# Query rounding split over two slices, gated tiles rounded inside the last attention slices, and two TensorE blocks set earlier, in a three-layer attention kernel

## The reference

```python
# layer 1 (A): windowed attention, 16 heads, context tokens too
q, k, v, g = split(h @ w_in)
q = apply_rope(q, cos, sin)            # image tokens only
p = softmax(concatenate([q @ k_window, q @ k_context, sink]))
y = ((p @ v) * silu(g)) @ w_o
# layer 2 (B): latent attention, 16 heads over all 768 keys
y = ((softmax((qn @ kn + qr @ kr) * scale) @ v) * silu(g)) @ w_o
# layer 3 (C, D): neighbourhood attention and an mLSTM, then w_out and the last norm
```

## Time and profile before

| what | us |
|---|---|
| median of 3 runs | 1173.31 |
| lowest, highest | 1172.9, 1174.43 |
| the profiled execution, its own time | 1174.93 |
| its span in the trace | 1173.1 |
| TensorE busy in it | 1105.2 |
| VectorE, ScalarE, GpSimd busy | 722.0, 652.3, 416.3 |

### The profile page before, as it was taken

One profiled execution on the slowest core, in us unless ns is written; L12 is line 12 of the kernel. 1 busy time (PEld: TensorE's weight loads), 2 busy tenths in 40 slices (PEclk: granted clock), 3 DMA queues, 4 the chain that ended last, 5 costly groups with the idle time before them and its releaser, 6 DMA issues.

```text
span 1173.1 us, 20182 instructions
## 1 busy us (share of the span) xinstructions
PE 1105.2 (94%) x7408; PEld 900.7 (77%) x7408; DVE 722.0 (62%) x1582; ACT 652.3 (56%) x1363; POOL 416.3 (35%) x512
## 2 busy tenths in 40 slices
PE   4899999999998899999999999999999999999896
PEld 0578788877886589887688888798778778887685
DVE  6365666676558625363787787645867774526545
ACT  4614455555556525643677778746567653447633
POOL 1633112211120333676400002316644335446871
PEclk9999999999989999999999999999999999999998
DMA  9741343423113621131201101043211404214112
GB/s 359 267 138 60 132 148 130 159 98 110 46 28 142 220 90 37 37 108 37 56 13 35 64 10 46 8 157 91 67 58 65 149 19 144 74 54 126 37 36 72
DMA packets 34253, 109.33 MB, mean 93 GB/s; under 512 B 4516, under 2 KB 7076, under 8 KB 33772
## 3 DMA queue, kind: packets, MB, share of 16 engines
q1 hardware_dynamic: 34156, 108.05, 27.6%
HBM read 101.39 MB, written 2.11 MB: 88 GB/s over the span
## 4 chain that ended last, share of the span: by engine, by line
PE 78%; DVE 9%; ACT 4%; issue 3%; POOL 3%; DMA 2%; SPq 0%; DVEq 0%; POOLq 0%; ACTq 0%
PE PS L675 32%; PE PS L658 15%; PE PS L791 8%; PE PS L779 7%; PE PS L970 6%; PE PS L1034 3%; PE PS L710 2%; PE PS L875 1%; DMA AF<-wstream 1%; POOL AR L2511 1%; DVE AF L2037 1%; DVE AD L2333 1%; PE PS L1009 1%; PE PS L691 1%; ACT AF L1257 1%
## 5 line engine op out<-in xcount | busy, mean ns | idle before, releaser
L2511 POOL TENSOR_TENSOR AR<-AF,AR 128x256 fp32r<-128x256 f32 x396 | 299.9, 792 | 601.0 <-ACT AR L1134 600.9
L675 PE MATMUL PS<-AR 128*128 128x512 f32 (+1 forms) x2208 | 452.3, 361 | 9.9 <-POOL AR L2511 4.1
L675 PEld LDWEIGHTS PS<-AR 128*128 128x128 f32 x2208 | 365.2, 190 | 78.0 <-issue 16.5
L658 PE MATMUL PS<-AR 128*128 128x256 f32 (+4 forms) x1284 | 246.4, 328 | 5.9 <-ACT AF L1257 1.7
L658 PEld LDWEIGHTS PS<-AR 128*128 128x128 f32 (+1 forms) x1284 | 181.0, 191 | 41.0 <-issue 20.8
L1266 ACT ACTIVATE AF<-PS 128x512 f32<-128x512 f32 (+3 forms) x192 | 124.5, 649 | 107.3 <-PE PS L779 103.3
L1257 ACT ACTIVATE AF<-PS,AF 128x512 f32<-128x512 f32 (+3 forms) x192 | 140.8, 734 | 22.0 <-DVE AF L2310 13.1
L779 PE MATMUL PS<-AF 128*128 128x128 f32 x864 | 127.8, 275 | 9.2 <-DVE AF L1958 5.8
L1134 ACT ACTIVATE AR<-AF 128x1024 fp32r<-128x1024 f32 x99 | 103.4, 1052 | 42.1 <-PE PS L970 27.8
L779 PEld LDWEIGHTS PS<-AF 128*128 128x128 f32 x864 | 100.3, 140 | 33.7 <-issue 15.1
L791 PE MATMUL PS<-AF 128*64 128x128 f32 x1728 | 115.6, 279 | 1.7 <-DVE AF L1965 1.7
(11 more groups left out here) (212 smaller groups left out, 1132.2 us busy)
## 6 DMA issues: line engine op xcount, KB each, us to landing
AF<-wstream SPq DMA_DIRECT2D x171, 512.0 KB, 4.8
AF<-x_in SPq DMA_DIRECT2D x2, 1024.0 KB, 8.1
AD<-rows SPq DMA_DIRECT2D x4, 512.0 KB, 5.9
out<-AF SPq DMA_DIRECT2D x16, 128.0 KB, 1.9
AF<-AF SPq DMA_DIRECT2D x28, 64.0 KB, 2.0
AF<-rpb_band SPq DMA_DIRECT2D x8, 224.0 KB, 5.0
BIAS<-rpb_band SPq DMA_DIRECT2D x8, 224.0 KB, 4.7
AF<-ctx_in SPq DMA_DIRECT2D x1, 1024.0 KB, 4.9
```

Of the source, the lines that this page charges most:

```text
L658: mm = pe.matmul(out, stationary, moving, start=i == 0, stop=i == len(products) - 1)
L675: mm = pe.matmul(out[:, 0:t1 - t0], a, b, start=k == 0 and i == 0, stop=k == nk - 1 and i == 2)
L2511: ins = pool.tensor_tensor(w[:, 1, at:at + 256], raw(c)[:, at:at + 256], w[:, 0, at:at + 256].bitcast(F32), ALU.subtract)
```

## The change

Five edits, in program order.

1. `ada_rows(0, 4)` on TensorE stands ahead of the fifth tile of the keys (k = 4), not behind it.
2. In layer 1, `split_image(p)` rounds the 512 image columns of the queries in `later` of slice 2, right behind `rope_q`; `split_q` of slice 3 rounds the 256 context columns alone. Pair 0 is as before.
3. At the end of layer 1's attention the first seven tiles of `A.o0.0` stand ahead of the last tile of `A.o0.1`, and the wait for the last `o_read` behind both.
4. At the end of layer 2's attention ScalarE and VectorE round the image columns' second half (part 1) of tiles 0 to 6 inside the last slices, and tile 7 and part 0 behind the last gate; TensorE starts `B.o0.1` without waiting for the last `o_read`.
5. In the iteration behind the last slice (`m == m1`), in layers 2 and 3 too, the values of the slice before are weighed between the two turnings, not behind them.

```diff
-                    if values_first and m0 <= m - behind - 1 < m1:
+                    ahead = values_first or m == m1
+                    if ahead and m0 <= m - behind - 1 < m1:
                         weigh_values(m - behind - 1)
...
-            project_together(keys, h_ready(0), 2, 5)
+            project_together(keys, h_ready(0), 2, 4)
             ada_rows(0, 4)
-            project_together(keys, h_ready(0), 5, KD)
+            project_together(keys, h_ready(0), 4, KD)
...
-            attend(0, A_END, ready_a, lambda m: fillers_a(m // 6 + 1, m % 6), values_first=True)
+            attend(0, A_END, ready_a, lambda m: fillers_a(m // 6 + 1, m % 6), values_first=True, drained=False)
+            project("A.o0.0", "A.o0", OA, 0, H, k1=KD - 1)
             make("A.o0.1:78")
-            project("A.o0.0", "A.o0", OA, 0, H)
+            project("A.o0.0", "A.o0", OA, 0, H, k0=KD - 1)
+            pe.wait_ge(o_read, group_of[A_END - 1] + 1)
...
+            def feeds_b(m):
+                if m == B_END - 2:
+                    act.wait_ge(s_ready, 2 * B_END)
+                    for j in range(2):
+                        out_high_b(j, 1)
+                if m == B_END - 1:
+                    for j in range(2, KD - 1):
+                        out_high_b(j, 1)
...
+            def split_query(p, at):
+                for half, h in enumerate(ROWS_OF):
+                    ins = dve.tensor_copy(QA[h, p % 2, half, at], QP[h, at])
+                step(ins)
+                return [dve.tensor_tensor(QA[ROWS_OF[1 - half], p % 2, half, at], QP[h, at],
+                                          QA[h, p % 2, half, at].bitcast(F32), ALU.subtract)
+                        for half, h in enumerate(ROWS_OF)]
+
+            def split_image(p):
+                dve.wait_ge(rope_sum, ropes[0])
+                if p >= 2:
+                    dve.wait_ge(s_ready, pair_scored("A", p - 2))
+                split_query(p, slice(0, S))
...
-                    dve.tensor_tensor(QA[ROWS_OF[1 - half], p % 2, half, :], QP[h, :],
-                                      QA[h, p % 2, half, :].bitcast(F32), ALU.subtract).then_inc(q_lo, 1)
+                split_query(p, slice(S, T) if p else slice(0, T))[1].then_inc(q_lo, 2)
...
                 elif s == 2:
                     rope_q(p)
+                    split_image(p)
...
+            def later_b(m):
+                if m == B_END - 1:
+                    for j in range(KD - 1):
+                        out_low_b(j, 1)
+
+            attend(A_END, B_END, others_b, later_b)
+            out_low_b(KD - 1, 1)
```

More of the change, by code:

```diff
@@ L820, in attend @@
                         turn(2 * (m - behind) + 1)
-                    if not values_first and m0 <= m - behind - 1 < m1:
+                    if not ahead and m0 <= m - behind - 1 < m1:
                         weigh_values(m - behind - 1)
@@ L944, in _ @@
             attend(A_END, B_END, ready_b,
-                   lambda m: fillers_b((m - A_END) // 4 + 1, (m - A_END) % 4) if (m - A_END) // 4 + 1 < N_PAIR else [])
+                   lambda m: fillers_b((m - A_END) // 4 + 1, (m - A_END) % 4) if (m - A_END) // 4 + 1 < N_PAIR else [],
+                   drained=False)
             for j in range(KD):
@@ L949, in _ @@
                     project("B.o0.0", "B.o0", OB, 0, H, ready=out_ready(16))
+                    pe.wait_ge(o_read, group_of[B_END - 1] + 1)
             for j in range(1, KD):
@@ L1441, in evacs_b, with out_high_b @@
                     need("B.o0", m - A_END - 23)
[L1443 to L1447, removed]
+            def out_high_b(j, part):
+                act.wait_ge(o_read, 16 + j + 1)
+                out_high("B", j, OB, [(OG[:, :, PART[part]], part * H, part * H + H)])
+            def feeds_b(m):
[6 more added lines that the diff above has]
+                        out_high_b(j, 1)
+            attend(A_END, B_END, evacs_b, feeds_b)
+            out_high_b(KD - 1, 1)
+            for j in range(KD):
+                out_high_b(j, 0)
             def squares_2(part, j):
@@ L2149, in others_b, with out_low_b @@
                         ada_part(name) if name.startswith("ada") else low_b(name)
-            attend(A_END, B_END, others_b)
-            step(dve.tensor_tensor(GAINF, GAIN[:, 2, :, 0], col("fg", 0, KD), ALU.mult))
[L2154 to L2159, removed]
+            def out_low_b(j, part):
+                dve.wait_ge(og_hi, 8 + (1 - part) * KD + j + 1)
+                dve.tensor_tensor(OB[1][:, j, PART[part]], OG[:, j, PART[part]], OB[0][:, j, PART[part]].bitcast(F32),
+                                  ALU.subtract).then_inc(og_lo, 1)
+            def later_b(m):
[4 more added lines that the diff above has]
+            out_low_b(KD - 1, 1)
+            step(dve.tensor_tensor(GAINF, GAIN[:, 2, :, 0], col("fg", 0, KD), ALU.mult))
+            for j in range(KD):
+                out_low_b(j, 0)
             def update_2(part, j):
```

## The result

The changed kernel takes 1190.08 us (median of four executions: 1185.03, 1189.24, 1190.91, 1191.03) against 1173.23 us for the kernel before on the same chip: a ratio of 1.0134, with a 95% interval of 1.0120 to 1.0149. It is slower by 16.9 us. The forecast was 1185.0, in a range of 1178 to 1191. The profiled execution was the quickest of the four, 1185.03 us with a span of 1183.2; the profiled execution of the kernel before took 1174.93, so the two traces hold 10.1 us of the loss. The others ran at lower granted clocks.

The account below looks back on a forecast made before the run. TensorE was taken to bound the kernel, so only its standing time counts. Edit 2 +12.1, edit 3 -1.1, edits 4 and 5 -2.0, edit 1 -0.1, clock +2.8 give +11.7 on 1173.31: 1185.0 us, range 1178 to 1191.

Parts of the forecast that it names:

- What bounds the kernel: TensorE holds 78% of the chain, VectorE 9%; time counts only where TensorE stands still or waits for another engine.
- Edit 2, the stall: Layer 1, pairs 1 to 5: rounding ahead of the modulation block's read delays each gate product 2.3 us, 11.5 in all.
- Pairs 6 and 7: Layer 1, gate in halves: the next maximum comes 0.2 to 0.5 us later in each pair, 0.6 us together.
- Edit 3: End of layer 1's attention: 21 products fill TensorE's 1.13 us wait; -1.1 us, bounds -0.8 and -1.1.
- Edits 4 and 5: End of layer 2's attention: output products start at 759.65 instead of 761.88; -2.0 us, bounds -1.2 and -2.3.
- none over 0.3: Sign in the changed trace: behind layer 2's attention TensorE shows no gap over 0.3 us.
- Edit 1: At the start, the 2.03 us wait for GpSimd reappears one tile later; -0.1 us, bounds -1.0 and 0.
- The clock: Behind the five gate waits, two clock falls at 1.4 us each: +2.8 us, bounds 0 and 13.5.
- the prediction's own case: Stall in full at the gates with one to three clock falls: 1183 to 1188 us, chance 0.44.
- nearly every gap brings a fall: Rival: the clock falls behind nearly every gate gap, or falls are long; 1189 to 1196 us, chance 0.17.
- half the stall: Rival: only about 1.2 us a pair stay ahead of the gates; 1177 us, chance 0.08.
- no loss: Rival "Faster": VectorE's insertion is hidden and edits 1, 3 and 4 remain; 1170 us, chance 0.06.

Follow-up runs that it names:

- changed, first: Profile of the changed kernel with all five edits, quickest of its first four executions: 1185.03 us, against 1174.93 for the profiled execution of the kernel before.
- changed, second: The changed kernel run again unaltered (empty diff) and profiled: an execution of 1192.6 us; that group's median was 1188.05 us, ratio 1.0114 to the kernel before.
- changed, third: The changed kernel run once more, unaltered, for one more profile: a single execution of 1187.76 us.

## Why the prediction was right in its steps, and where a size was off

**What bounds the kernel** held: the loss is time in which TensorE stands, and TensorE's own work is unchanged.

**Edit 2, the stall.** Predicted 2.3 us a pair, a wait of 2.4 to 2.6 us in place of 0.20. Measured: 2.34 to 2.36 us in each of the five pairs, from casts of 0.43 each and subtractions of 0.69 or 0.70. That every inserted microsecond moves the product is shown by the kernels with less and with more of it, and that it is the place and not the work by the one with the rounding behind the read. The removal from slice 3 saved nothing in those pairs, as said. Pairs 6 and 7: predicted 0.6 us together, and a wait of about 1.9. Measured 1.86 us ahead of pair 6's scores (1.67 before). What the pairs lost in all is told by the **offset**: the start of an instruction in the changed kernel's trace less its start in the trace of before. In pair 6 it grows by 0.25 us, from 13.01 (319.32 to 332.33) to 13.26 (326.12 to 339.38). In pair 7 it grows by 0.58 us, from 12.15 to 12.73, between these two rows of before, which answer to 370.43 and 377.49:

```profile
358.28 3.00 PE L675 MATMUL PS<-AR 128*128 128x512 f32 x12
...
364.76 1.91 PE L710 MATMUL PS<-AF 128*12 128x512 f32 x16 [1.34 <-DVE AF L1933]
```

So 0.8 us together, with pair 7 just above the 0.5 that bounded each. There VectorE stood 0.44 us ahead of its first cast, and 0.09 in pair 6.

**Edit 3.** Predicted -1.1. In the trace the offset falls by 1.36 us across the layer's end (from 12.43 at the last fillers to 11.07 at 475 us of before); alone it brought 2.1 us by the median, with the lower bound at 0.8. That is more than the bound of 1.1 allowed. The 1.13 us are counted from the end of the last product to the next start; from start to start, the six products and the gap took 2.79 us (404.53 to 407.32), and six of these products take some 1.4 us, an estimate from 5.74 us for 24 and 3.00 for 12. So about 1.4 us were there to be won.

**Edits 4 and 5.** Predicted -2.0. In the trace the offset falls from 10.70 (753.07 to 763.77) to 8.86 (761.88 to 770.74), 1.84 us; alone they brought 2.2 us. One of the signs was put badly: "none over 0.3" overlooks the copy of the last turning, which the working itself had ahead of the last weighing, and which is the remaining 0.90 us.

**Edit 1.** Predicted -0.1, with a gap of about 2.2 us ahead of tile 5. The gap was 1.79, 2.17 and 2.17 us in the three profiles, and TensorE left the start 1.5 us earlier, 1.5 later and 0.9 later than in the profile of before (61.51, 64.54 and 63.99 against 63.05). The first profile alone would have called the edit a gain of 1.5 us. By its own run it changes the time by something between -2.2 and +0.6 us. What the argument lacked is the fall of the clock behind this gap too, 1.5 us in two profiles of three; the prediction had taken the clock at full speed there from the one profile of before.

**The clock** is the term that was mis-sized. Predicted were two falls in five gates at 1.4 us: 2.8 us. The first profile had this (2.9 us). But it was the quickest of its group, and that its 1185.03 us meet the forecast of 1185.0 is luck: the forecast was of the median, and the start was 1.5 us early in that one execution. The three profiles have 2, 4 and 2 falls behind the five gates, 8 of 15, and one of them cost 2.8 us: 2.9, 7.4 and 2.9 us. The Trainium skill, TensorE: Matmul & The Clock Gate, Part 1, has the monitor run free of the kernel, so that executions of one program differ; the traces agree, with gaps equal to 0.01 us and unequal falls.

**The sum.** Without the clock it is +12.1 - 1.1 - 2.0 - 0.1 = +8.9 by the prediction. By the traces edits 2 to 5 are 11.7 + 0.8 - 1.4 - 1.8 = +9.3. The rest differs from profile to profile (us, against the profile of before; the kernel with edit 2 alone has no -1.4 and -1.8):

| profile | edits | falls at the gates | start | clock at pair 6 | rest | measured |
|---|---|---|---|---|---|---|
| changed, first | 9.3 | 2.9 | -1.5 | -1.1 | 0.5 | 10.1 |
| changed, second | 9.3 | 7.4 | 1.5 | -1.1 | 0.6 | 17.7 |
| changed, third | 9.3 | 2.9 | 0.9 | -1.1 | 0.8 | 12.8 |
| edit 2 alone | 12.5 | 3.0 | -0.8 | -1.1 | 1.0 | 14.6 |

The column of pair 6 is the old fall of the earlier trace rows, which lasted less long than in the profile of before in all four: the offset drops by 1.1 us behind it (from 13.26 to 12.14 in the first). The prediction had -2.7 for its vanishing, among the bounds only. The rest is what remains: in the first profile two groups of products near the end of layer 3 took 1.2 us longer, with no edit near, and 0.7 us came back elsewhere. The last two columns, which the prediction's sum did not have, cancel in large part.

The medians (+16.9 and +15.3 us in the two groups) lie 6 to 8 us above the edits' 9.3, where the prediction had 2.8 for the clock; this is most of the 5 us between 1185.0 and 1190.08. That the unprofiled executions owe theirs to falls is argued, not shown. In the first group the mean granted clock falls as the time grows (1185.03 at 0.989, 1189.24 at 0.986, 1190.91 at 0.982, 1191.03 at 0.980), but in the later one executions of 1185.12 and 1192.6 us both have 0.985. The median of 1190.08 also lies outside the prediction's own case (1183 to 1188), near the upper end of its range and inside the band of the rival "nearly every gap brings a fall" (1189 to 1196); the falls lie between the two, 8 in 15 gaps and 4.4 us in the mean of three profiles.

The rivals of half the stall and of no loss are refuted: waits of 1.2 us came only when half the insertion was taken out. Left open is how much of edit 1's interval is its own, and why the kernel with only the casts ahead had a median of 1176.41, 3.2 us above its profiled execution of 1173.2, in which no gate product was slow. That one profile also has no fall behind pair 6 (granted clock 1.00 there), which took 0.9 to 2.7 us in every other; this may be part of the 3.2, and is not shown.

## What to carry to other kernels

Before an instruction is moved ahead on an engine that has time to spare, look for what stands behind it there: if that is the read which frees a bank or buffer for the bounding engine, and that engine already waits for it by however little, the whole inserted length is added each time round; behind the read the same work was free here, because the gate product covered it. A gap put into TensorE's stream can cost more than its length, by an amount that differs between executions, so such a term wants a range of its own and more than one profile. An offset seen in a single pair of profiles (the 1.5 us at the start) is no gain until several profiles, or the times of the edit alone, show it.

## What the runs showed of the hardware

- At a full-rate stream of 24 products of 512 columns (5.73 to 5.78 us), gaps of 1.25 to 1.95 us brought a fall in none of 5 (one profile, of the quickest of ten executions), gaps of 2.54 to 3.24 us in 10 of 20 (four profiles, the kernel with edit 2 alone among them), and gaps of 3.43 to 4.48 us in 5 of 5 (one profile).
- A fall cost 1.4 to 1.6 us in nine of those ten and 2.8 us in one. Behind the longest gaps it cost 1.6 to 2.8 us. One and the same gap at the start, 2.17 to 2.19 us, was followed by 6.56 us in one profile and by 8.09, 8.09 and 8.11 us in three others.
- The length of a gap does not decide alone. In pair 6, among smaller products, one gap of 1.67 us was followed by a fall in each of five profiles, and one of 1.12 us by a fall too (rounding behind the read, granted clock 0.76 over the 7 us behind it), but one of 1.62 us by none (only the casts in slice 2). From those scores to the second half of the gate product TensorE took 8.43 us without the fall and 9.29 to 11.14 us behind the gap of 1.67, so the fall cost 0.9 to 2.7 us.
- At the end, the gap of 3.04 us for GpSimd was there before and after (3.03 at 1104.55); two groups of products behind it, 0.73 and 1.88 us before, took 1.09 and 2.69 us in the changed kernel's first profile, without any edit near. Over all profiles the second group took 1.53 to 2.69 us.
